# Down weights of experts 4 to 63 loaded from ScalarE's queue at the end of its step

## The reference, cut to what matters

```
idx, w = route(xf, w_router, bias)              # 8 of 64 experts for each token
for each expert e, with its tokens:             # D = 1024, D_EXPERT = 256
    y = (silu(x @ w_gate[e]) * (x @ w_up[e])) @ w_down[e] * w
    sum[tokens] += y
y = sum + shared expert(x);  h = layer_norm(alpha * h + y)
```

## Time and profile before

| | |
|---|---|
| median of 3 runs | 2449.37 us (2445.22 to 2451.26) |
| the profiled execution's own time | 2451.56 us |
| its span, first to last instruction | 2449.7 us |
| mean granted TensorE clock | 0.949 of full speed; 1.00 in the windows shown below |
| busy: PE / PE loads / VectorE / ScalarE / Pool | 2210.4 / 1679.8 / 1598.6 / 1259.7 / 457.5 us |
| moved in all | 536.68 MB, 457.50 MB of it by SP's queue |

### The profile page before, as it was taken

The page is one execution under the profiler, slowest core; times in us unless marked ns, Lnnn a source line. Parts: engine busy times, 40 slices in busy tenths (PEclk is TensorE's granted clock), DMA queues, the critical chain, the costliest instruction groups (busy, mean ns, idle before and its releaser), DMA issues. The chain is left out here.

```text
span 2449.7 us, 36342 instructions
## 1 busy us (share of the span) xinstructions
PE 2210.4 (90%) x10361; PEld 1679.8 (69%) x10361; DVE 1598.6 (65%) x2553; ACT 1259.7 (51%) x2072; POOL 457.5 (19%) x343
## 2 busy tenths in 40 slices
PE   7989688877999999999999399999999998999992
PEld 6867667776667776777777265567676776777771
DVE  3768754455578877788777321434777777888883
ACT  3332122122347777787776112322477776777871
POOL 0000322230013322232222000000132222322220
PEclk9999899998999999999999599699999999999996
DMA  5221000000469999999998502013699999999993
GB/s 190 87 86 39 18 1 1 1 1 19 173 225 376 373 360 348 359 376 367 361 357 289 172 26 69 1 39 132 230 366 340 365 351 342 372 364 372 372 348 94
DMA packets 177844, 536.68 MB, mean 219 GB/s; under 512 B 25856, under 2 KB 55520, under 8 KB 177632
## 3 DMA queue, kind: packets, MB, share of 16 engines
q1 hardware_dynamic: 147568, 457.50, 49.5%
q0 software_dynamic: 25248, 69.25, 11.3%
q10 hardware_dynamic: 4944, 8.84, 1.0%
HBM read 501.56 MB, written 54.07 MB: 227 GB/s over the span
## 5 line engine op out<-in xcount | busy, mean ns | idle before, releaser
L1322 DVE TENSOR_TENSOR gu_l<-ring,gu_h 128x1024 fp32r<-128x1024 f32 x512 | 611.3, 1221 | 99.5 <-ACT gu_h L1208 90.6
L1208 ACT CAST gu_h<-ring 128x1024 fp32r<-128x1024 f32 x512 | 523.3, 1058 | 91.7 <-DMA ring<-in_moe_w_up 74.3
L1140 PE MATMUL bank<-gu_h,xgT_l 128*128 128x512 f32 x1024 | 413.5, 404 | 0.0
L1142 PE MATMUL bank<-gu_h,xgT_h 128*128 128x512 f32 x1024 | 401.7, 392 | 0.0
L1141 PE MATMUL bank<-gu_l,xgT_h 128*128 128x512 f32 x1024 | 400.7, 391 | 0.0
L1450 POOL DMA_INDIRECT xg<-h_rows,list_idx x128 | 143.4, 1120 | 836.7 <-issue 318.2
L1179 PE MATMUL bank<-ring,hmT_f 128*128 128x512 f32 x544 | 279.3, 595 | 0.0
L1468 POOL DMA_INDIRECT moe_sum<-y,out_idx x128 | 216.1, 1688 | 220.2 <-issue 212.7
L1215 ACT CAST down_h<-ring 128x1024 fp32r<-128x1024 f32 x130 | 136.2, 1047 | 213.4 <-PE bank L1179 116.2
L1328 DVE TENSOR_TENSOR down_l<-ring,down_h 128x1024 fp32r<-128x1024 f32 x130 | 159.4, 1226 | 99.9 <-ACT down_h L1215 97.9
L1142 PEld LDWEIGHTS bank<-gu_h,xgT_h 128*128 128x128 f32 x1024 | 193.2, 189 | 42.6
(11 more groups left out here) (301 smaller groups left out, 3531.3 us busy)
## 6 DMA issues: line engine op xcount, KB each, us to landing
ring<-in_moe_w_gate SPq DMA_DIRECT2D x256, 512.0 KB
ring<-in_moe_w_up SPq DMA_DIRECT2D x256, 512.0 KB
ring<-in_moe_w_down SPq DMA_DIRECT2D x256, 512.0 KB
ring<-in_a_w_in SPq DMA_DIRECT2D x32, 512.0 KB
ring<-in_a_w_out SPq DMA_DIRECT2D x8, 512.0 KB
h_rows<-ring ACTq DMA_DIRECT2D x8, 512.0 KB, 2.7
moe_sum<-y ACTq DMA_DIRECT2D x8, 512.0 KB, 7.4
ring<-moe_sum SPq DMA_DIRECT2D x8, 512.0 KB, 5.5
```

Of the source, the lines that this page charges most:

```text
L1140: nc.tensor.matmul(out, lhsT=xl, rhs=wh, start=k == 0, stop=False)
L1142: last = nc.tensor.matmul(out, lhsT=xh, rhs=wh, start=False, stop=k == KD - 1)
L1208: nc.scalar.copy(gu_h[:, c, :, :], gate_up_cols(gate_slot, c * CH // 2, CH // 2)).then_inc(gu_hi.sem, 1)
L1322: nc.vector.tensor_tensor(gu_l[:, c, :, :], gate_up_cols(gate_slot, c * CH // 2, CH // 2), gu_h[:, c, :, :].bitcast(F32), ALU.subtract).th ...
```

## The change

`load_unit` moves out of SP's program and takes the engine as an argument. SP loads gate and up of all experts, and down of experts 0 to 3. ScalarE issues the down load of expert r + 3 at the end of its step r, behind `act_result` of r - 1, from r = 1 on; the last one is that of expert 63 in step 60. The wait for the slot, the two DMAs of 512 KB each and their semaphores are the same.

```diff
@@ act_step
                 if r >= 1:
                     act_result(act, r - 1, i)
+                    if not last:
+                        load_down(act, r + 3, i)
                 else:
                     act_store_sum(act, TT - 1)
@@ before steps(); the same body as before, with eng for sp
+            def load_unit(eng, r, i, j):
+                n = U + 3 * r + j
+                if slot_free(n):
+                    used, value = slot_free(n)
+                    eng.wait_ge(used.sem, value + 4 * (CH_GU if j < 2 else 1) * i)
+                for h in range(2):
...
+            def load_down(eng, r, i):
+                load_unit(eng, r, i, 2)
@@ SP's program
-                    load_gate_up(0, 0)
+                    load_gate_up(sp, 0, 0)
                     for r in range(4):
-                        load_gate_up(r + 1, 0)
-                        load_down(r, 0)
+                        load_gate_up(sp, r + 1, 0)
+                        load_down(sp, r, 0)
                     with sp.Fori(0, LOOP) as i:
                         for r in range(4, 8):
-                            load_gate_up(r + 1, i)
-                            load_down(r, i)
+                            load_gate_up(sp, r + 1, i)
                     for r in range(E - 4, E - 1):
-                        load_gate_up(r + 1, 0)
-                        load_down(r, 0)
-                    load_down(E - 1, 0)
+                        load_gate_up(sp, r + 1, 0)
```

More of the change, by code:

```diff
@@ L1476, in pool_step, with load_gate_up @@
                     pool_scatter(pool, r - 1, i)
+            weights = [a[w][layer].rearrange("e (p k) c -> e p (k c)", p=P) for w in ("moe_w_gate", "moe_w_up", "moe_w_down")]
+            def load_unit(eng, r, i, j):
[4 more added lines that the diff above has]
+                for h in range(2):
+                    w, c0 = (weights[h], j * HALF) if j < 2 else (weights[2], h * HALF)
+                    eng.dma_start(ring[:, slot_of(n), h * HALF:(h + 1) * HALF], w[bass.ds(r + 4 * i, 1), :, c0:c0 + HALF].rearrange("e p c -> (e p) c")).then_inc(slot_loaded[slot_of(n)].sem, 16)
+            def load_gate_up(sp, r, i):
+                load_unit(sp, r, i, 0)
+                load_unit(sp, r, i, 1)
+            def load_down(eng, r, i):
+                load_unit(eng, r, i, 2)
             def steps(eng, step):
```

## The result

| | before | after |
|---|---|---|
| median | 2450.32 us (2445.22 to 2452.59, 4 runs) | 2509.37 us (2494.38 to 2518.20, 4 runs) |
| ratio | | 1.0238, 95% interval 1.018 to 1.0295 |
| profiled execution: time, span | 2451.56, 2449.7 us | 2518.20, 2516.3 us |
| granted clock, mean | 0.949 | 0.941 |

The change costs 59 us by the medians (66.6 by the two profiled spans: the profiled execution of after is the slowest of its four). The direction and the range of the prediction held; its 2480 us had the loss at half its size. In the kernel after, lines behind L1330 keep their order but carry other numbers: the gather is L1452, the scatter L1470, every weight load L1490.

A forecast was written before the change was run, and what follows sets the result against it. Bound taken: the two-step loop through the token gather, 9.93 us a step, beside nearly full DMA engines. A gather 0.9 us longer gives +0.23 us a step, +28.5 us on 2451.56: 2480 us, range 2436 to 2535.

The forecast's parts named there:

- Two resources nearly full: Experts' stretches: PE busy 95.2 and 99.9 of 100 us, DMA engines' share 1.01 and 1.02; which sets the step?.
- Removed from SP: nothing: SP's program: two issues and one wait fewer in each of 60 experts a layer, costed at nothing because its queue is full.
- rival C: Experts' steps: down weights arrive two steps early, PE's stops before hm go, 28.2 us faster, 2424 us; chance 0.17.
- Added on ScalarE: nothing: End of ScalarE's step: wait, two issues and register work, about 1 us, hidden behind two y activations; 0 on the path.
- Rival D: ScalarE after y: its issues wait while SP's queue is full, 0.8 us a step, 99 us, about 2550 us; chance 0.12.
- Moved, and what it costs the gather: Pool's gather beside down loads on a second queue: 0.9 us longer, bounds 0 and 3.3 us.
- my own formula: Two-step gather loop: 12.34 us turn to gather, 7.51 gather to turn, 0.9 added; 20.75 us, 10.38 a step.
- Weight waits then no longer add to it: Experts' steps: the longer step gives weight loads more time, so late weights add nothing to 10.38 us a step.
- Rival B: Layer end: only load order changes, expert 63's gate and up land 5 us later a layer, say 2457 us; chance 0.20.

The follow-up runs named there:

- before_early: Kernel before with VectorE's two small list copies moved up, so the gather is issued some 4 us earlier in the step; 2446.8 us, ratio 0.999.
- after_r2: Changed kernel with ScalarE issuing down weights of expert r+2 instead of r+3, same queue and place in the step; 2493.6 us, ratio 1.0167.
- after_early: Changed kernel with VectorE's two small list copies moved up, so the gather is issued some 4 us earlier in the step; 2488.4 us, ratio 1.0168.
- after_r2_early: Changed kernel with down weights issued for expert r+2 instead of r+3 and the gather issued some 4 us earlier; 2465.8 us, ratio 1.0087.
- half: Changed kernel with ScalarE loading only the first 512 KB of each expert's down weights, SP the second in the old order; 2480.5 us, ratio 1.0118.
- after_early_tail: Changed kernel with the gather issued earlier and down weights of a layer's last four experts back on SP's queue; 2475.9 us, ratio 1.0102.
- one_queue_ahead1: Kernel before, all weights on SP's queue, with down one expert further ahead in SP's order; 2458.4 us, ratio 1.0036.
- one_queue_ahead: Kernel before, all weights on SP's queue, with down two experts further ahead in SP's order; 2505.1 us, ratio 1.0215.

## Why the prediction was right in direction and half too small

**Two resources nearly full.** Right, and both had a part in the loss. The loop through the gather, (12.34 + 7.51) / 2 = 9.93 us a step by one row each, and the DMA engines' own work, 1254.5 / 124 = 10.12 us a step, lay 0.2 us apart. But my sentence that the gather is already on the path was wrong: before_early took it away and gained nothing that can be measured. In the kernel before the DMA engines set the pace, and the gather had a little slack: by the events it landed 0.54 and 0.73 us before PE's turn in the median.

**Removed from SP: nothing.** Nothing speaks against it, and no run tests it alone. What I didn't price is that the moved loads arrive 20 us earlier than before, although rival C counted on it. The half of this that after_r2 takes back costs 16 to 23 us by the medians (after against after_r2, after_early against after_r2_early), 11.6 to 18.4 by the stretches. By which way is open: ScalarE's waits for up don't show it (86.9 + 73.2 us in after_early, 78.2 + 92.3 in after_r2_early).

**Added on ScalarE: nothing.** Right. The issue takes 0.34 us in the median, at most 0.51 in layer 0, where SP stands up to 8.7 us in one of its own, and 0.79 in layer 1. Rival D's premise, that a full SP queue would hold up ScalarE's for 2 us and more, is refuted by these rows.

**Moved, and what it costs the gather: the term that was mis-sized.** I put the gather at 0.9 us longer. From the semaphore events of the gathers in both traces, their last part lands on average 6.97 us after the start in layer 0 before (60 gathers) and 8.00 us after; in layer 1 6.92 and 8.77 us (the view of the gather's line gives medians of 7.7 and 8.9 for after). The increase is 1.0 and 1.85 us. Put into my own formula, (12.34 + 7.51 + 1.0) / 2 = 10.43 and (12.34 + 7.51 + 1.85) / 2 = 10.85 us a step; measured 10.45 and 10.83. So in layer 0 the term was about right, and in layer 1 it was twice what I took: there most of the missing 30 us lies (40.7 us of growth against the forecast's 14). The two legs of the loop bear this out. From PE's turn to the gather that follows from that step, the mean was 12.54 and 12.59 us before and 12.28 and 12.36 after, so that leg didn't grow; from the gather to PE's turn it was 7.69 and 7.83, then 8.69 and 9.42.

But that the formula comes out doesn't show that the gather alone made the steps long. In after_early no gather holds PE, and layer 0 still takes 10.39 us a step, layer 1 10.48. And in half the formula would give (12.34 + 7.51 + 0.13) / 2 = 9.99 us for layer 0, where 10.35 were measured. One premise of the term was visibly off: I had the down load land in 5 to 6 us, at half of the engines; the page of after gives 9.1 us in the median (10.3 and 11.2 us for the second of the two issues, by the events), so that it lies over nearly all of the gather.

```profile
ring<-in_moe_w_down ACTq DMA_DIRECT2D x240, 512.0 KB, 9.1
```

The Trainium skill ("DMA: Bandwidth & Descriptors", "Queues, rings and completion order") has each engine go round all queues with work. With q0 as the third, an estimate by that rule is a third of 417 GB/s for the load while a gather runs, 7.5 us for 1.05 MB and the start on top; the row agrees better with that than with my half.

**"Weight waits then no longer add to it."** In the changed kernel this held for PE in layer 1 (one stop for hm, 5.2 us) and less so in layer 0 (12.0 us). What failed is what it was used for: to put down the whole loss to the gather. I let the longer step give the loads time. after_early shows that the weights, too, are later than before: with no stop for a gather it still took 38 us more than the kernel before. The DMA engines needed 1273.0 us for the bytes that took 1251.6 us in before_early (shares of 98.6% of 644.2 and 98.2% of 649.5 us, against 99.9% of 623.8 and 99.7% of 630.3), and had nothing to do for 20.7 us instead of 2.5.

**Rival B.** I had it as another outcome; it is a term that adds. In after_early the last weights land 10.3 and 10.8 us ahead of the silu of expert 63, in the kernel before 3.6 and 3.8: 13.7 us more in which the engines have no weights to load. after_early_tail, where they land 7.8 and 9.8 us before it, was faster by 12.5 us by the medians and 7.0 by the experts' stretches; I gave this at most 10. **Rival C** did its part: the waits for down went, hm's stops shrank by 11 us, and the gather's swallowed it.

**A cost that I left out: the clock.** PE's 12.7 us of longer busy time go with its clock. In layer 1 PE stood 5.23 us for hm, and the window over its end has PE at 0.50 of full speed, 1.2 GHz of 2.4. The timeline and the window:

```profile
1831.69 0.69 PE L1152 MATMUL bank<-const,hm 128*128 128x128 f32 x2 [5.23 <-DVE hm L1305]
```

```profile
1830.00:1834.00 4.00, 2.31 (x11) 2.27 (x12) 3.85 (x6) 3.77 (x6) 0.00 (x0) 0.50 1.02 411
```

By the clock records of the traces, PE was at the lower level for 10.2 us in the experts' stretches before and for 44.4 us after, and it was busy for 10.1 and 40.6 us of these. At the higher level half of the 30.5 us more would be gone, an estimate of 15 us, against the 12.7 measured. Ahead of each of these falls PE had stood still, for 2.0 to 5.2 us. A stop of PE can so be paid a second time.

**Sum.** By the medians of the experiments: gather 21 us (28 when down arrives 10 us later), half of the early arrival 16 to 23, end of the layers up to 12.5. By the experts' stretches: 25.7 (18.9), 11.6 to 18.4, 7.0. That leaves 19 us by the medians and 28.0 by the stretches between after_r2_early and before_early, of which the end of the layers and the other 10 us of early arrival are a part; with a single queue as much early arrival cost 8 us (one_queue_ahead1). What remains goes with the DMA engines needing 1268.6 us instead of 1251.6 for the same bytes. I called it Q, the price of a second queue, but one_queue_ahead had 1287.6 us with a single queue. one_queue_ahead also had its gathers land in 7.30 and 7.49 us, so a part of their delay doesn't need a second queue either. So why the packets take 1 to 3% longer in the slower kernels stays open, as does why the gather suffers twice as much in layer 1.

## What to carry to other kernels

When two resources lie within a few per cent of each other, take each off the path in an experiment of its own before you say what bounds, and add the rivals' prices: here three costs came together, the gather's, the early arrival's and the end of a layer's, and I had priced one and named another as an alternative. A load that is moved to another queue is also moved in time: ask separately beside which small, late-needed transfer it now runs, how long it holds its buffer, and which load now comes last. Asking for it as late as before doesn't make it arrive as late, if its new queue is faster. Remedies made for the same loss don't add up either; trace them together before you count on it.

## What the runs showed of the hardware that I had not expected

- A DMA issue on ScalarE's queue took 0.33 to 0.79 us (240 of them a run, 0.34 in the median), while SP's took up to 8.7 us in layer 0. Long issues on one queue didn't hold up those of the other.
- With a megabyte a step on a second queue the gathers beside it took 1.0 us (layer 0) and 1.85 us (layer 1) longer; with half a megabyte (half) 0.1 and 0.2 us (7.10 and 7.11 us, by the same count as above). It isn't proportional.
- The same megabyte landed 10.3 and 11.2 us after its second issue on ScalarE's queue, where nothing stood ahead of it; on SP's, behind gate and up, it took 19.4 and 18.8 us.
- Two DMAs of 4 KB in each step, 17,280 packets a layer, cost 11 us in a kernel whose DMA engines are full.
